# Products with values of two attention heads on the two column halves of TensorE

## The reference

```python
# first block, second layer: dilated window attention, 3 groups, 16 heads of 64
scores = jnp.einsum('bnqrhd,bnkrhd->bnrhqk', qb, kk) * (HEAD_DIM ** -0.5)
scores = jnp.where(valid, scores + bias, NEG_INF)
p = jnp.exp(scores - lse[..., None])
out = jnp.einsum('bnrhqk,bnkrhd->bnqrhd', p, vv)
...
return (merged * jax.nn.silu(gate)) @ w_out
# second block: compressed, selected and window branch, 16 heads on 4 key/value groups
s = jnp.einsum('bgnqd,bgkd->bgnqk', qb, k_cmp).astype(jnp.float32) * scale - slopes * d_c
p_cmp = masked_softmax(s, d_c >= 0)
o_cmp = jnp.einsum('bgnqk,bgkd->bgnqd', p_cmp.astype(v_cmp.dtype), v_cmp)
```

## Time and profile before

| | before |
|---|---|
| median of 3 runs | 3589.13 us (3587.99 to 3591.36) |
| profiled execution, its own time | 3583.92 us |
| its span | 3582.2 us |
| TensorE busy | 3403.4 us, 95% |
| VectorE, ScalarE, GpSimd busy | 45%, 30%, 43% |
| mean granted clock of TensorE | 0.974 |
| first block's attention, units 0 to 63 | 528.8 to 1046.2 us |
| second block's 64 units | 1276.7 to 1864.8 us |

### The profile page before, as it was taken

The page is one execution under the profiler, slowest core; times in us unless marked ns, Lnnn a source line. Parts: engine busy times, 40 slices in busy tenths (PEclk is TensorE's granted clock), DMA queues, the critical chain, the costliest instruction groups (busy, mean ns, idle before and its releaser), DMA issues. The chain is left out here.

```text
span 3582.2 us, 40618 instructions
## 1 busy us (share of the span) xinstructions
PE 3403.4 (95%) x14972; PEld 2549.9 (71%) x14972; DVE 1608.7 (45%) x2751; ACT 1062.9 (30%) x2006; POOL 1531.3 (43%) x873
## 2 busy tenths in 40 slices
PE   8999999999969999999999999988999899889998
PEld 7886987777743867777448878775555688668886
DVE  4742003333332045554320153433788789737741
ACT  2112013233314134344330011355666400321111
POOL 6764653333311433433026656660001166446664
PEclk9999999999979989999999999999999899999999
DMA  4233221111104211211452323231111122223221
GB/s 158 96 99 112 95 83 59 59 54 59 59 24 153 83 54 62 71 62 62 147 173 97 115 78 105 89 99 48 53 48 48 42 95 94 68 68 100 95 95 58
DMA packets 84487, 297.19 MB, mean 83 GB/s; under 512 B 9441, under 2 KB 10977, under 8 KB 84162
## 3 DMA queue, kind: packets, MB, share of 16 engines
q1 hardware_dynamic: 80352, 286.34, 24.0%
q10 hardware_dynamic: 3250, 5.77, 0.5%
q0 software_dynamic: 688, 2.49, 0.2%
HBM read 289.32 MB, written 2.10 MB: 81 GB/s over the span
## 5 line engine op out<-in xcount | busy, mean ns | idle before, releaser
L596 POOL TENSOR_SCALAR arena_r<-ring 128x1024 fp32r<-128x1024 f32 x430 | 463.6, 1078 | 1913.5 <-PE psum L608 1293.3
L606 PE MATMUL psum<-arena_r,arena_r 128*128 128x512 f32 (+2 forms) x3120 | 1235.7, 396 | 36.4 <-DVEq L2952 13.4
L607 PE MATMUL psum<-arena_r,arena_r 128*128 128x512 f32 (+2 forms) x3120 | 1204.2, 386 | 0.0
L608 PE MATMUL psum<-arena_r,ring_r 128*128 128x512 f32 (+1 forms) x3088 | 1193.1, 386 | 0.0
L598 POOL TENSOR_TENSOR ring_r<-ring,arena_r 128x1024 fp32r<-128x1024 f32 x430 | 1057.6, 2460 | 64.6 <-issue 10.0
L606 PEld LDWEIGHTS psum<-arena_r,arena_r 128*128 128x128 f32 x3120 | 592.5, 190 | 178.5 <-issue 43.7
L607 PEld LDWEIGHTS psum<-arena_r,arena_r 128*128 128x128 f32 x3120 | 592.6, 190 | 121.0 <-issue 9.9
L608 PEld LDWEIGHTS psum<-arena_r,ring_r 128*128 128x128 f32 x3088 | 583.0, 189 | 118.4
L1141 DVE SCALAR_TENSOR_TENSOR arena<-arena,con,psum 128x512 f32<-128x512 f32 x64 | 47.8, 747 | 450.7 <-PE psum L1088 450.7
L2328 PE MATMUL psum<-arena,ring 128*128 128x512 f32 x512 | 234.8, 603 | 14.6 <-ACT arena L2403 14.5
L2328 PEld LDWEIGHTS psum<-arena,ring 128*128 128x128 f32 x512 | 94.6, 194 | 114.6 <-issue 114.6
(11 more groups left out here) (389 smaller groups left out, 4233.8 us busy)
## 6 DMA issues: line engine op xcount, KB each, us to landing
ring<-in_weights SPq DMA_DIRECT2D x534, 512.0 KB, 3.3
arena<-arena ACTq DMA_DIRECT2D x20, 128.0 KB, 3.3
arena<-in_x_t SPq DMA_DIRECT2D x8, 256.0 KB, 4.9
out_t<-arena SPq DMA_DIRECT2D x8, 256.0 KB, 2.2
arena<-in_w_ck POOLq DMA_DIRECT2D x1, 1024.0 KB, 8.7
arena<-in_w_cv POOLq DMA_DIRECT2D x1, 1024.0 KB, 10.9
arena<-in_ln_bc ACTq DMA_DIRECT2D x1, 1024.0 KB
arena<-in_ctx_t ACTq DMA_DIRECT2D x1, 1024.0 KB, 7.3
```

Source lines behind the costliest of these rows:

```text
L596: nc.gpsimd.tensor_scalar(hi_part(t), src, 1.0, 1.0, ALU.mult, ALU.mult)
L606: nc.tensor.matmul(out, w_hi, a_hi, start=start, stop=False)
L607: nc.tensor.matmul(out, w_hi, a_lo, start=False, stop=False)
L608: return nc.tensor.matmul(out, w_lo, a_hi, start=False, stop=stop)
```

## The change

In both attentions the products with values of the two heads of a pair are issued alternately, one for partitions 0 to 63 and one for 64 to 127 of the output bank, each pair of them with the same key chunk. For that the probabilities of both heads must be there at once:

- First block: `unit` lets the heads alternate (even units the first head, odd units the second, r = u // 2). The products with values are issued in odd units only, for both heads. The near products of both heads come in unit 7. The turned probabilities have their own tiles for each head, and the values change places (`v_at`) so that tiles come free for the second half of the pairs. `pv_done` counts four a pair.
- Second block: the order of units stays. The products with values come once a pair, in unit 7, for both heads; the compressed part of the second head is in two products of 256 columns, since its probabilities lie in two pieces. The second head's turned probabilities go to tiles 40 to 44, where the first five gate tiles (`g0`) were written. So these five tiles leave the slots and stand at the head of the list behind the loop, and unit 7 of the pairs 3 to 7 has no job. The other jobs move up.
- ScalarE waits for the products with values of the pair before at unit 0, and in the first block from n = 4 on for those of the units two to four before.

```diff
     rest = [(n, m) for m in range(KT) for n in ("cg", "xin", "cb", "cz")]
-    rest += [("g0", m) for m in range(5)] + [("mod", g) for g in range(12)]
+    rest += [("mod", g) for g in range(12)]
...
-                slots.append(rest.pop(0))
-    post = [("g0", m) for m in range(5, KT)] + [(n, m) for n in ("g1", "br0", "br1", "gv", "u", "gz", "g2", "br2", "o")
+                slots.append(None if u == 7 and p >= 3 else rest.pop(0))
+    post = [(n, m) for n in ("g0", "g1", "br0", "br1", "gv", "u", "gz", "g2", "br2", "o")
                                                for m in range(KT)]
...
-                near_t = tiles(60, 2).rearrange("p a (b r n) -> p (a b) r n", b=2, n=64)
-                far_t = [arena[:, 62 * S + b * 256:62 * S + (b + 1) * 256] for b in range(2)]
+                def near_t(p, off):
+                    at = 60 if off == 0 else 69 if p < 4 else 8
+                    return tiles(at, 2).rearrange("p a (b r n) -> p (a b) r n", b=2, n=64)
+                def far_t(n):
+                    p, off, r = unit(n)
+                    at = (62 if off == 0 else 68 if p < 4 else 10) * S + 256 * (r % 2)
+                    return arena[:, at:at + 256]
...
-                    return p, 64 * (u // 4), u % 4
+                    return p, HD * (u % 2), u // 2
...
                         pe.wait_ge(pt_done, n + 1)
-                        if n % UN == 0 and p > 0:
+                        if n % 2 == 0:
+                            continue
+                        if n % UN == 1 and p > 0:
                             pe.wait_ge(gate_done, p)
-                        pos = P * (p % 4) + off
+                        pos = P * (p % 4)
                         for g in (1, 2):
-                            last = nc.tensor.matmul(psum[off:off + HD, 7, r::4], v_at(g, r, p // 4)[:, pos:pos + HD],
-                                                    far_t[n % 2][:, (g - 1) * P:g * P], start=(r == 0 and g == 1), stop=False,
-                                                    skip_group_check=True)
+                            for off in (0, HD):
+                                last = nc.tensor.matmul(
+                                    psum[off:off + HD, 7, r::4], v_at(g, r, p // 4)[:, pos + off:pos + off + HD],
+                                    far_t(n - (off == 0))[:, (g - 1) * P:g * P], start=(r == 0 and g == 1), stop=False,
+                                    skip_group_check=True)
...
-                        if r == 0 and n:
-                            act.wait_ge(pv_done, n)
-                        elif n >= 2:
-                            act.wait_ge(pv_done, n - 1)
+                        if r == 0 and p:
+                            act.wait_ge(pv_done, 4 * p)
+                        elif n >= 4:
+                            act.wait_ge(pv_done, n // 2 - 1)
...
                         pe.wait_ge(pt_done, n + 1)
-                        if n % UN == 3 and p:
+                        if n % UN < 7:
+                            continue
+                        if p:
                             pe.wait_ge(gate_done, p)
-                        if i == 3:
-                            nc.tensor.matmul(psum[off:off + HD, 6], vcmp[:, HD * g:HD * (g + 1)], prob_c, start=True,
-                                             stop=False, skip_group_check=True)
-                            for c in range(4):
-                                for kind, first in ((0, 4 * c), (1, 16 - 3 * c)):
-                                    v_c = 256 * kind + HD * g
+                        g_a, g_b = g - 1, g
+                        nc.tensor.matmul(psum[0:HD, 6], vcmp[:, HD * g_a:HD * g_b], prob_c, start=True, stop=False,
+                                         skip_group_check=True)
+                        for part in range(2):
+                            nc.tensor.matmul(psum[HD:P, 6, 256 * part:256 * (part + 1)], vcmp[:, HD * g_b:HD * (g_b + 1)],
+                                             prob_b[part], start=(part == 0), stop=False, skip_group_check=True)
+                        for c in range(4):
+                            for kind, first in ((0, 4 * c), (1, 16 - 3 * c)):
+                                for half, to in ((0, g_a), (1, g_b)):
+                                    v_c = 256 * kind + HD * to
                                     last = nc.tensor.matmul(
-                                        psum[off:off + HD, 6, c * P:].rearrange("p (b n) -> p b n", n=P),
-                                        v_all[:, c, v_c:v_c + HD], prob_t[:, first:first + 4 - c], start=False,
+                                        psum[HD * half:HD * (half + 1), 6, c * P:].rearrange("p (b n) -> p b n", n=P),
+                                        v_all[:, c, v_c:v_c + HD], prob_ts[half][:, first:first + 4 - c], start=False,
                                         stop=(c == 3 and kind == 1), skip_group_check=True)
-                            last.then_inc(pv_done, 1)
+                        last.then_inc(pv_done, 1)
```

More of the change, by code:

```diff
@@ L957, in v_at @@
                 def v_at(g, j, half):
-                    i = (g * 4 + j) * 2 + half
+                    i = 12 * half + 4 * g + j
                     return tiles(8 + i if i < 16 else 32 + i, 1)[:, 0]
@@ L1121, in _ @@
                                 w = 64 if c < 3 else 32
-                                last = nc.tensor.matmul(
-                                    psum[off:off + HD, 7, c * P:c * P + 4 * w].rearrange("p (i r) -> p r i", r=4),
-                                    v_at(0, c, p // 4)[:, pos:pos + HD], near_t[:, c, :, 0:w],
-                                    start=False, stop=(c == 3), skip_group_check=True)
+                                for off in (0, HD):
+                                    last = nc.tensor.matmul(
+                                        psum[off:off + HD, 7, c * P:c * P + 4 * w].rearrange("p (i r) -> p r i", r=4),
+                                        v_at(0, c, p // 4)[:, pos + off:pos + off + HD], near_t(p, off)[:, c, :, 0:w],
+                                        start=False, stop=(c == 3), skip_group_check=True)
                         last.then_inc(pv_done, 1)
@@ L1488, in hybrid_block, with kind_of @@
                 row_in, turned, g0_in = sem("n_row_in"), sem("n_turned"), sem("n_g0_in")
-                mod_no = {job: i for i, job in enumerate([j for j in slots if j[0] == "mod"])}
+                mod_no = {job: i for i, job in enumerate([j for j in slots if j and j[0] == "mod"])}
+                prob_ts = [prob_t, tiles(40, 5).rearrange("p a (b n) -> p (a b) n", n=P)]
+                prob_b = [arena[0:N_CMP, at_b:at_b + 256] for at_b in (60 * S + 256, 62 * S + 7778)]
+                def kind_of(n):
+                    return slots[n][0] if 0 <= n < NU and slots[n] else None
                 def unit(n):
@@ L1534, in _ @@
                             qk(n + 2)
-                        if n and slots[n - 1][0] == "mod":
+                        if kind_of(n - 1) == "mod":
                             mod_turn(pe, mod_no[slots[n - 1]], row, 2, 7, row_in, turned)
-                        if job[0] == "mod":
+                        if kind_of(n) == "mod":
                             mod_group(pe, at[job], c3, 2, 7)
-                        else:
+                        elif job is not None:
                             tile_columns(pe, at[job], 7, h_hi, h_lo)
@@ L1553, in _ @@
                                         stop=(c == 3 and kind == 1), skip_group_check=True)
-                            last.then_inc(pv_done, 1)
-                    if slots[-1][0] == "mod":
+                        last.then_inc(pv_done, 1)
+                    if kind_of(NU - 1) == "mod":
                         mod_turn(pe, mod_no[slots[-1]], row, 2, 7, row_in, turned)
@@ L1607, in _ @@
                         act.wait_ge(tr_done, n + 1)
-                        if i == 0 and n:
-                            act.wait_ge(pv_done, n // 4)
-                        nc.scalar.activation(prob_c[:, i * P:(i + 1) * P], psum[0:N_CMP, 3, 0:P], ACT.Copy)
+                        if n % UN == 0 and n:
+                            act.wait_ge(pv_done, p)
+                        c_to = prob_b[i // 2][:, i % 2 * P:(i % 2 + 1) * P] if off else prob_c[:, i * P:(i + 1) * P]
+                        to_t = prob_ts[off // HD]
+                        nc.scalar.activation(c_to, psum[0:N_CMP, 3, 0:P], ACT.Copy)
                         turned_p = psum[:, 4:6].rearrange("p a (b n) -> p (a b) n", n=P)
-                        nc.scalar.activation(prob_t[:, i:4 * i + 1:3], turned_p[:, 0:i + 1], ACT.Copy)
-                        nc.scalar.activation(prob_t[:, 16 - 3 * i:17 + i:4], turned_p[:, i + 1:2 * i + 2], ACT.Copy)
+                        nc.scalar.activation(to_t[:, i:4 * i + 1:3], turned_p[:, 0:i + 1], ACT.Copy)
+                        nc.scalar.activation(to_t[:, 16 - 3 * i:17 + i:4], turned_p[:, i + 1:2 * i + 2], ACT.Copy)
```

(9 more changed lines are left out.)

12 lines of the change are left out of this document (7 added, 5 removed).

## The result

| | before | after |
|---|---|---|
| median | 3589.39 us | 3536.35 us (4 runs, 3535.23 to 3541.43) |
| ratio, 95% interval | | 0.9857 (0.9845 to 0.987) |
| profiled execution, its own time | 3583.92 us | 3541.43 us |
| its span | 3582.2 us | 3539.7 us |
| TensorE busy | 3403.4 us | 3341.1 us |

A forecast was written before the change was run, and what follows sets the result against it. TensorE's queue order was taken as the bound, except in the first block's last pair. Terms -26.9 - 43.6 + 0.6 + 8.2 = -61.7 us gave 3522.2 us profiled, 3527.4 us median; range 3514 to 3550.

The forecast's parts named there:

- -43.6 products: Second block: products with values once a pair instead of once a head, removing 8 x 5.45 = 43.6 us; 0 without overlap.
- +1.7 copies: Second block's emptied unit 7: TensorE waits for ScalarE's probability copies, some 0.6 us in pair 3, 1.0 in pair 4.
- Full overlap: Both attentions: products on the two column halves run side by side, four passes taking 0.37 us, not 0.58; chance 0.78.
- (a): Rival: halves run one behind the other, as weights and data differ or by the skill's rule; 3590 us, chance 0.09.
- (b): Rival: no overlap, and each of some 330 turns between halves costs about 0.1 us; 3622 us, chance 0.04.
- (c): Rival: half the overlap, as two different fp32 moving operands run at a reduced rate; 3563 us, chance 0.07.
- spacing of 0.107 us: TensorE's time between passes of 128 columns, used to derive full overlap; larger spacings were to show the forecast wrong.
- First block: Filled units of pairs 0 to 6: even units and unit 3 save 3.84 us a pair, 26.9 us in all.
- Unit 7 at nothing: First block's unit 7: both heads' near products overlap, hidden by the wait on VectorE's normalization; saves nothing.
- A last pair longer than 61 us: Sign that the forecast is wrong: the first block's last pair, expected to save nothing, lasts longer than 61 us.
- Gate tiles: Five tiles moved behind the second block's loop: gain 1.1 us, emptied slots wait on ScalarE; net cost 0.6, bounds 0 and 3.
- The xin waits: Second block: TensorE waits on VectorE's convolution, three times 2.0 us and once 2.2, sum 8.2; bounds 0 and 12.

The follow-up runs named there:

- the second profile of the changed kernel: The changed kernel run again, nothing altered: median 3533.96 us, 0.9842 of before, profiled execution 3533.14 us.
- the run with the halves in turn: Changed kernel with all products with values of one head issued first, then all of the other, in both blocks: 3579.04 us, 0.9971 of before.
- the kernel without the taps: Changed kernel without VectorE's two passes for the last two taps of the short convolution: 3507.76 us, 0.9773 of before.
- the run with the other form of the normalization: Changed kernel with VectorE's second-block normalization written as scalar_tensor_tensor instead of tensor_scalar: 3541.85 us, 0.9868 of before.

## Why the prediction was right, and where 9 us went

Stages are taken from the second profile of the changed kernel, near its median: the loop begins at 1246.76 and lasts 544.0 us, and 1740.6 us lie behind it.

```profile
1246.76:1790.80 544.04, 519.56 (x2476) 345.23 (x2476) 272.59 (x642) 218.72 (x642) 163.98 (x94) 0.97 0.29 96
1790.80:3531.40 1740.60, 1636.40 (x7184) 1257.76 (x7184) 944.50 (x1481) 524.57 (x795) 797.22 (x450) 0.97 0.24 79
```

| | forecast | measured |
|---|---|---|
| up to the loop | -26.9 | -30.0 |
| the loop | -62.0 (-43.6 products, -28.3 tiles, +1.7 copies, +8.2 xin) | -44.0 |
| behind it | +27.2 (5 x 5.44) | +23.2 |
| span | -61.7 | -50.8 |

*Full overlap.* Right. Rows 9 were one instance with shared operands; different weights, different data and accumulation change nothing. Rivals (a), (b) and (c) are out: the value group is 5.47 us, and the run with the halves in turn loses what the overlap was said to bring in the second block. In the first block the mechanism was right and the reason half right: side by side, but not because the heads alternate.

The prediction's spacing of 0.107 us is slightly low: passes of 128 columns start 0.109 us apart in before, and 0.160 for the second of a group. That leaves 0.36 instead of 0.37, and the conclusion stands; but spacings above 0.107 could not have been a sign of being wrong.

*First block.* Forecast 26.9; by the first profile 30.3 in seven pairs and 0.9 given back in the last. Even units last 7.63 us instead of 7.70, odd ones 8.25 instead of 8.28 and unit 7 is 0.05 shorter: together some 0.4 a pair, 2.9 for seven, and the very first unit gives some 0.3 more, in the first profile only. Unit 7 at nothing: right (5.22 against 5.27). In the last pair TensorE is at the low clock a unit sooner, as the bound said. The transposes of the second unit still take 0.85 us, but the scores behind them 1.24 instead of 0.81, and that unit is 8.65 us instead of 7.86; the pair takes 62.6 us instead of 61.7. In the second profile that unit is 8.35 us and the pair only 0.2 us longer. "A last pair longer than 61 us" was no sign of being wrong, since before's own has 61.7.

*Gate tiles.* Right in kind (the prediction's own terms, 0.6 + 1.0 - 1.1, give 0.5, not 0.6). In a unit without a tile the products wait for ScalarE's copies (timeline of after, pair 3, unit 7):

```profile
1516.92 0.64 PE L1568 MATMUL psum<-arena 31*64 31x512 f32 x1 [0.57 <-ACTq L1643]
```

That is 0.57 us for a forecast of 0.6. In pair 4 it is the same, not 1.0.

Behind the loop 4.0 us were gained that the forecast hasn't. Counted back from the end, TensorE's records in before and in the changed kernel drift apart at two places above all. The wait on ScalarE behind the `gv` tiles (line 1888 in before) is 2.25 us in before and in the run with the first block alone, and 0.78 us in every kernel with the tiles moved:

```profile
2057.69 0.47 PE L606 MATMUL psum<-arena_r,arena_r 128*128 128x512 f32 x1 [2.25 <-ACT arena L1888]
```

```profile
2009.47 0.47 PE L606 MATMUL psum<-arena_r,arena_r 128*128 128x512 f32 x1 [0.78 <-ACT arena L1918]
```

The banks there go to the tiles in turn, four of them, and five more tiles shift the turn by one; that this is why the wait is shorter was not tested. Another 1.6 us are clock: behind line 1819 the granted clock is 0.51 in before (2326.5 to 2329.8 us) and 1.00 at the same place of the changed kernel (2278.2 to 2280.0).

*The xin waits: the step that failed.* Place, cause and count were right: three units of 2.0 and one of 2.2, 8.2 us. Measured against their old periods they are 3 x 4.17 + 4.36 = 16.9, outside the bound of 12 as well. The forecast took the 5.44 us of the convolution from the earlier trace rows as VectorE's own. In that trace too one tap of the two had taken 2.75 us instead of 0.75 (VectorE, before):

```profile
1398.43 2.75 DVE L1673 SCALAR_TENSOR_TENSOR arena<-arena,par 128x512 f32<-128x512 f32 x1
```

So the sum carried one hold unseen; the second came with the change. Behind an xin in unit 3 or 4, without products with values in between, GpSimd's next subtraction has just begun when VectorE, late, comes to its normalization. The latter is then held for another 2 us, and that goes straight to TensorE. In before the longest normalization of the second block was 1270 ns; at these four places it is 2427 to 2507. (One of 2564 ns in the last unit, where no xin is near, stands in the kernel without the taps too, with 2562.) The prediction had a bound of 12 "should GpSimd's work stretch VectorE's", in a clause, without asking in the trace whether it did.

*What had no term.* In the profiles of before and the two of the changed kernel TensorE's clock stays after 1.85 us of waiting in five instances of six, and after 4.0 to 4.2 us it falls in all eight (over all traces: three falls in 14, and 21 in 21). The units behind the four waits last 8.99, 10.27, 9.17 and 10.07 us instead of 7.41, 7.41, 7.06 and 7.41: 9.2 us, and one more unit 1.7 (unit 7 of pair 5, 10.00 us instead of 8.31). That last one isn't tied to the waits: three kernels without them have it in pair 6. Waits 8.7 above the forecast, clock 10.9, copies 0.5 below: 19.1, for 18.0 that are missing in the loop. The total came nearer than the loop's term partly by luck: 3.1 us in the first block and 4.0 behind the loop, neither foreseen, went the other way.

The Trainium skill, on the page "SBUF — State Buffer", section "SBUF: two separate sides", says what the runs say: VectorE and GpSimd have one pair of ports in common, the instruction that gets it first keeps it to its end, and a VectorE instruction with two inputs in SBUF needs it against a GpSimd instruction that reads there. The taps and the rewritten normalization have two such inputs and are held (2.74 and 2.56 us), front has one and isn't (0.61), and a fill that only writes holds no tap. For the normalization as it was, with one input, the page names a mode in which VectorE takes both pairs; it was held for 2 us as well, and its time fits such a mode (0.50 ns a column, from 407 ns for 256 columns and 536 for 512, against 1.03 for the two-input form with 479 and 744). With that rule and two rows's stretch, VectorE's and GpSimd's, the hold could have been read before the change was made.

The rule on weight loads that the prediction set against the change, from "TensorE: Matmul & The Clock Gate", section "The mechanism" of part 3, isn't borne out here: both halves have the same rows of the array, and they overlap in full; as in the earlier trace rows, the weights of the second passes (from 1321.40 us) are loaded while the first passes of line 1577 (1321.34 to 1321.99) run on both halves.

## What to carry to other kernels

Small products for the two column halves ran side by side at full worth here, in the first block even with two of one half ahead of two of the other; with longer runs alternate them. When work leaves the bound engine's queue, list what it had covered, and read the cover's price operation by operation: a merged row whose mean is twice the usual may hide one instruction that was held. Where GpSimd and VectorE are released by the same event, move those of VectorE's operations on SBUF that are held by a few microseconds, or cut GpSimd's instruction into pieces: here either was worth half as much as the change itself.

## What of the hardware had not been expected

TensorE runs products of the two column halves together even where those of one half stand ahead in the queue: two products of one half and then two of the other take 0.67 us, as if alternated (0.66). With four each it was 2.60 us, against 1.68 alternated: the second half began when two of the first half's products were left. Between the last products of 128 rows and the first of 31 rows no overlap was seen (10.90 = 2 x 5.45).

A subtraction on GpSimd that lasts 2.40 us holds a VectorE operation of 0.75 us for 2.0 us more; in eight pieces of together 4.31 us it holds no tap for more than 0.12 (they take 789 to 873 ns). A fill with zeros of 0.95 to 1.06 us at the same place holds none at all (750 to 754 ns). GpSimd is held too: in before its pass of line 596 takes 1.31 us instead of 1.05 where a normalization of 512 columns runs.

A wait of 4 us on TensorE costs about 6: the wait, and 1.5 to 3.1 us in the unit behind it at the 1.2 GHz level, in all 21 instances of six traces (4.0 to 4.5 us of waiting). Waits of 1.85 us cost that in three of 14 instances of seven traces: once in the first profile (unit 7 of pair 1, 14.53 us instead of 12.97), and in both instances of the run with the second block alone (14.56 and 10.79 us instead of 12.97 and 7.95). The two of 2.27 us in the run with the other form of the normalization cost it both times (14.54 and 10.54). What decides in the short ones the runs don't show.
